# Rounding rows as they come, and three barriers fewer, in layer 1 and block 2 of a two-block transformer kernel

## The reference, cut to what matters

```
br_a = ((a_b * _short_conv(a_c * a_x, conv_w_l)) * silu(a_z)) @ w_br_conv_l
...
return (g_a * br_a + g_b * br_b + g_c * br_c) @ w_out_l
```

```
y = einsum('nbsm,nmd->bsnd', branches, w_branch[layer])
x = x + sum(gate * y, axis=2) @ w_out[layer]
```

## Time and profile before

| | |
|---|---|
| time, median of 3 runs | 4196.48 us (4193.07 to 4197.07) |
| profiled execution | 4197.54 us |
| its span, first to last instruction | 4195.7 us |
| mean granted TensorE clock | 0.955 |
| TensorE busy | 3878.6 us, 92% |
| VectorE, GpSimd, ScalarE busy | 1880.7, 1959.9, 974.4 us |
| layer 1's convolution begins, last matmul | about 2688, 2871 us |
| layer 1's branch product ends | about 2928 us |
| block 2's branch products end | about 3749 us |

### The profile page before, as it was taken

One profiled execution on the slowest core, in us unless ns is written; L12 is line 12 of the kernel. 1 busy time (PEld: TensorE's weight loads), 2 busy tenths in 40 slices (PEclk: granted clock), 3 DMA queues, 4 the chain that ended last, 5 costly groups with the idle time before them and its releaser, 6 DMA issues. The chain is left out here.

```text
span 4195.7 us, 52077 instructions
## 1 busy us (share of the span) xinstructions
PE 3878.6 (92%) x19691; PEld 3083.5 (73%) x19691; DVE 1880.7 (45%) x2716; ACT 974.4 (23%) x1729; POOL 1959.9 (47%) x834
## 2 busy tenths in 40 slices
PE   5999999999989989899999998898898998999999
PEld 4777788888877877576678777676585454877877
DVE  5344326656638882344425655355304555133200
ACT  3333212222210011333312222101214444112200
POOL 2333342332326554244454343687452210887886
PEclk7999999999999999899999999999898998999999
DMA  7211221121225543222222121334422110443433
GB/s 191 49 47 43 74 56 46 44 48 41 52 76 112 117 110 101 60 56 58 75 66 56 44 61 48 90 90 119 128 57 56 38 31 14 95 105 78 96 91 90
DMA packets 481706, 305.17 MB, mean 73 GB/s; under 512 B 37786, under 2 KB 451875, under 8 KB 480635
## 3 DMA queue, kind: packets, MB, share of 16 engines
q1 hardware_dynamic: 469434, 282.43, 28.0%
q10 hardware_dynamic: 12096, 20.33, 1.4%
HBM read 276.42 MB, written 26.27 MB: 72 GB/s over the span
## 5 line engine op out<-in xcount | busy, mean ns | idle before, releaser
L867 POOL TENSOR_TENSOR whi<-ring,con 128x1024 fp32r<-128x1024 f32 (+1 forms) x415 | 978.6, 2358 | 2180.6 <-DMA ring<-in_w_in 1681.4
L551 PE MATMUL ps<-xT_parts,whi 128*128 128x512 f32 (+2 forms) x2632 | 1007.1, 383 | 77.0 <-DVE hT_parts L2099 37.7
L551 PE MATMUL ps<-hT_parts,whi 128*128 128x512 f32 (+1 forms) x2864 | 1049.2, 366 | 0.0
L869 POOL TENSOR_TENSOR ring_parts<-ring,whi 128x1024 fp32r<-128x1024 f32 (+1 forms) x415 | 983.9, 2371 | 32.5
L551 PE MATMUL ps<-xT_parts,ring_parts 128*128 128x512 f32 (+2 forms) x2600 | 944.3, 363 | 0.0
L551 PE MATMUL ps<-arena_parts,whi 128*128 128x512 f32 (+1 forms) x2472 | 765.9, 383 | 74.2 <-DVE arena_parts L2093 63.2
L1551 ACT ACTIVATE arena<-ps 128x512 f32<-128x512 f32 (+7 forms) x583 | 311.5, 544 | 1671.2 <-PE ps L551 960.3
L551 PE MATMUL ps<-arena 128*128 128x128 f32 (+9 forms) x3292 | 647.7, 341 | 27.8 <-DVE arena L2061 22.1
L551 PEld LDWEIGHTS ps<-xT_parts,whi 128*128 128x128 f32 (+1 forms) x2632 | 500.3, 190 | 182.7 <-issue 64.3
L551 PEld LDWEIGHTS ps<-hT_parts,whi 128*128 128x128 f32 x2864 | 544.1, 190 | 91.1 <-issue 7.2
L551 PEld LDWEIGHTS ps<-arena_parts,whi 128*128 128x128 f32 x2472 | 460.0, 194 | 181.4 <-issue 73.9
(11 more groups left out here) (160 smaller groups left out, 3377.1 us busy)
## 6 DMA issues: line engine op xcount, KB each, us to landing
ring<-in_w_in SPq DMA_DIRECT2D x504, 256.0 KB, 4.0
arena<-in_w_ada SPq DMA_DIRECT2D x80, 256.0 KB, 6.2
ring<-in_w_up SPq DMA_DIRECT2D x64, 256.0 KB, 4.0
ring<-in_w_down SPq DMA_DIRECT2D x64, 256.0 KB, 3.6
ring<-in_w_out SPq DMA_DIRECT2D x48, 256.0 KB, 3.8
gates_kept<-stage ACTq DMA_DIRECT2D x24, 384.0 KB, 4.0
arena<-gates_kept SPq DMA_DIRECT2D x24, 384.0 KB, 3.7
ring<-in_w_br_attn SPq DMA_DIRECT2D x32, 256.0 KB, 3.9
```

Source lines behind the costliest of these rows:

```text
L551: return nc.tensor.matmul(o, l, r, start=first, stop=last)
L867: v.tensor_tensor(hi, raw, ones[:, 0:m].unsqueeze(1).to_broadcast([P, kt, m]), ALU.mult).then_inc(w_rounded, 1)
L869: v.tensor_tensor(ringR[:, s, 0:kt, 0:m], raw, hi.bitcast(F32), ALU.subtract).then_inc(w_split, 1)
```

## The change

In layer 1 and in block 2 the activation rows are rounded and subtracted one at a time, as they are made, by new calls in the loops that make them. The barriers `conv1`, `branch0_1` and `branches2` are left out on all engines. The two parts of acc get a place of their own, `acc2P`, in columns of con from `cos` on. VectorE and ScalarE do layer 1's convolution, and block 2's third branch, in written-out loops. SyncE's waits for the barriers become waits for an earlier barrier (gates) and for used weight tiles (x). Layer 0 stays as it is.

```diff
+        acc2P = parts(con[:, C_AT["cos"][0]:C_AT["cos"][0] + KT * LAT].rearrange("p (f n) -> p f n", f=KT), acc)
...
+        acc_row = sem("acc_row")
...
-            def bring_x(before, n, kept):
+            def bring_x(before, n, kept, used=None):
-                sp.wait_ge(phase, 3 * phases_to(before))
+                if before:
+                    sp.wait_ge(phase, 3 * phases_to(before))
+                else:
+                    sp.wait_ge(w_used, used)
...
-                branch(0, a["w_br_conv"][l], f"conv{l}")
+                branch(0, a["w_br_conv"][l], "conv0" if l == 0 else "branch2_1")
...
-                        bring_x(f"branch0_{l}", ALL, l + 1)
+                        bring_x("branch0_0" if l == 0 else None, ALL, l + 1, tiles.number() - 4)
...
-                    bring_x("branches2", LAT, 3)
+                    bring_x(None, LAT, 3, tiles.number() - 4)
```

TensorE:

```diff
-                if phase_end(f"conv{l}"):
+                if l == 0 and phase_end("conv0"):
                     return
                 branch(n)
-                if phase_end(f"branch0_{l}"):
+                if l == 0 and phase_end("branch0_0"):
                     return
-                summed_tiles(accP, n)
+                summed_tiles(accP if l == 0 else acc2P, n)
...
-            if phase_end("branches2"):
-                return
-            summed_tiles(accP, LAT)
+            summed_tiles(acc2P, LAT)
```

ScalarE (`gates_of_conv` is the body of the old loop, `gate2` that of block 2):

```diff
+                def round_row(dst, src, f):
+                    do(dst[0][:, f, 0:n], src[:, f, 0:n], ACT.Copy).then_inc(part_hi, 1)
+                if l == 0:
...
+                else:
+                    for f in range(KT):
+                        gates_of_conv()
+                        if f:
+                            round_row(yP, y, f - 1)
+                    last_read()
+                    round_row(yP, y, KT - 1)
+                    skip(KT)
+                    for f in range(KT):
+                        act.wait_ge(acc_made, KT * (BRANCH_AT[0] + 3 * l) + f + 1)
+                        round_row(acc2P, acc, f)
...
+            def round_row2(f):
+                act.wait_ge(acc_row, f + 1)
+                do(acc2P[0][:, f], acc[:, f, 0:LAT], ACT.Copy).then_inc(part_hi, 1)
+            for b in range(2):
                 with act.Fori(0, KT // 2) as i, tiles.loop(i, KT // 2, 4), uses.loop(i, KT // 2, 4):
                     for s in range(2):
+                        gate2()
+            for f in range(KT):
+                gate2()
+                if f:
+                    round_row2(f - 1)
+            round_row2(KT - 1)
```

VectorE (`conv_row` is the body of the old loop):

```diff
+            def row_rest(dst, src, f, n):
+                parts_made[0] += 1
+                dve.wait_ge(part_hi, parts_made[0])
+                v.tensor_tensor(dst[1][:, f, 0:n], src[:, f, 0:n], dst[0][:, f, 0:n].bitcast(F32),
+                                ALU.subtract).then_inc(part_lo, 1)
-            def branch(b, l, n):
-                keep_rest(yP, y, n)
+            def branch(b, l, n, by_rows=False):
+                if not by_rows:
+                    keep_rest(yP, y, n)
...
+                    if by_rows and f:
+                        row_rest(acc2P, acc, f - 1, n)
+                if by_rows:
+                    row_rest(acc2P, acc, KT - 1, n)
...
+                else:
+                    for f in range(KT):
+                        conv_row(f)
+                        if f:
+                            row_rest(yP, y, f - 1, n)
+                    row_rest(yP, y, KT - 1, n)
...
+            for f in range(KT):
+                skip()
+                p = product()
+                last_read()
+                own.settle()
+                dve.wait_ge(acc_row, f)
+                release(stt(tmp2, tha2, 1.0, bank(2 * p), ALU.add, ALU.mult))
+                last_read()
+                dst = acc[:, f, 0:LAT]
+                stt(dst, tmp2, 0.5, dst, ALU.mult, ALU.add).then_inc(acc_row, 1)
+                if f:
+                    row_rest2(f - 1)
+            row_rest2(KT - 1)
```

More of the change, by code:

```diff
@@ L73 @@
 PHASES = ["load"] + [f"{p}{l}" for l in range(DEPTH)
-                             for p in ("attn", "branch1_", "gla", "branch2_", "conv", "branch0_")] \
-    + ["kv2", "cmp", "heads", "branches2", "up", "down", "end"]
+                             for p in ("attn", "branch1_", "gla", "branch2_", "conv", "branch0_")[:6 if l == 0 else 4]] \
+    + ["kv2", "cmp", "heads", "up", "down", "end"]
 def phases_to(name):
@@ L1852, in _, with gates_of_conv @@
                     return
-                with act.Fori(0, KT) as i, tiles.loop(i, KT, 4), uses.loop(i, KT, 4):
+                def gates_of_conv():
                     p = product()
@@ L1860, in _ @@
                     skip(3)
[L1861 to L1866, removed]
+                def round_row(dst, src, f):
+                    do(dst[0][:, f, 0:n], src[:, f, 0:n], ACT.Copy).then_inc(part_hi, 1)
+                if l == 0:
+                    with act.Fori(0, KT) as i, tiles.loop(i, KT, 4), uses.loop(i, KT, 4):
+                        gates_of_conv()
+                    if phase_end("conv0"):
+                        return
+                    branch(n)
+                    if phase_end("branch0_0"):
+                        return
+                    round_rows(accP, acc, n)
+                else:
+                    for f in range(KT):
+                        gates_of_conv()
+                        if f:
[6 more added lines that the diff above has]
+                        round_row(acc2P, acc, f)
                 for f in range(KT):
@@ L2011, in _, with gate2 @@
             round_rows(y2P, y2, LAT)
-            for b in range(3):
+            def gate2():
+                p = product()
+                last_read()
+                release(do(tha2, bank(2 * p), ACT.Tanh, scale=0.5))
+                skip()
[3 more added lines that the diff above has]
+            for b in range(2):
                 with act.Fori(0, KT // 2) as i, tiles.loop(i, KT // 2, 4), uses.loop(i, KT // 2, 4):
                     for s in range(2):
[L2015 to L2021, removed]
+                        gate2()
[4 more added lines that the diff above has]
+            round_row2(KT - 1)
             for f in range(KT):
@@ L2418, in _, with conv_row @@
                 ns = len(stretches)
-                with dve.Fori(0, KT) as i, tiles.loop(i, KT, 4), uses.loop(i, KT, 4), own.loop(i, KT, 4 * ns + 16 * (l == 0)):
+                def conv_row(i):
                     if l == 0:
@@ L2460, in _ @@
                 if l == 0:
+                    with dve.Fori(0, KT) as i, tiles.loop(i, KT, 4), uses.loop(i, KT, 4), own.loop(i, KT, 4 * ns + 16):
+                        conv_row(i)
+                else:
[4 more added lines that the diff above has]
+                    row_rest(yP, y, KT - 1, n)
+                if l == 0:
                     dve.wait_ge(mod_read, KT)
@@ L2464, in _ @@
                     own(v.tensor_tensor(gpost[:], modl[:, 16:24], over(R_GPOST, 8), ALU.mult))
-                if phase_end(f"conv{l}"):
+                if l == 0 and phase_end("conv0"):
                     return
[L2467 to L2470, removed]
+                branch(0, l, n, l == 1)
+                if l == 0:
+                    if phase_end("branch0_0"):
+                        return
+                    keep_rest(accP, acc, n)
                 skip(8)
@@ L2669, in _, with row_rest2 @@
                             own(stt(dst, tmp2, 0.5, dst, ALU.mult, ALU.add))
-            if phase_end("branches2"):
-                return
+            acc2_from = parts_made[0]
+            parts_made[0] += KT
+            def row_rest2(f):
+                dve.wait_ge(part_hi, acc2_from + f + 1)
+                v.tensor_tensor(acc2P[1][:, f, 0:LAT], acc[:, f, 0:LAT], acc2P[0][:, f].bitcast(F32),
+                                ALU.subtract).then_inc(part_lo, 1)
+            for f in range(KT):
+                skip()
+                p = product()
+                last_read()
+                own.settle()
+                dve.wait_ge(acc_row, f)
+                release(stt(tmp2, tha2, 1.0, bank(2 * p), ALU.add, ALU.mult))
+                last_read()
+                dst = acc[:, f, 0:LAT]
[3 more added lines that the diff above has]
+            row_rest2(KT - 1)
             def residual():
@@ L2678, in _ @@
             add_at = [0]
-            keep_rest(accP, acc, LAT)
             dve.wait_ge(x_back, 48)
```

## The result

| | before | after |
|---|---|---|
| time, median of 4 runs | 4195.36 us (4193.07 to 4197.07) | 4169.89 us (4165.37 to 4172.04) |
| ratio, 95% interval | | 0.9936 (0.9922 to 0.9950) |
| profiled execution, its span | 4197.54, 4195.7 us | 4172.04, 4170.2 us |
| granted TensorE clock, mean | 0.955 | 0.959 |

A forecast was written before the change was run, and what follows sets the result against it. TensorE, busy 92% of the span, bounds the kernel, so gains lie in its standstills and low clock. 8.8 + 9 + 10.5 - 4.5 = 23.8 us off the 4196.5 us median gave 4172.7 us, range 4163 to 4185.

The forecast's parts named there:

- the clock: TensorE's clock falls in the remaining pauses: 2 us lost each at A and C, 0.5 at B, 4.5 together.
- A: Layer 1, convolution to branch product: the first tile, 18.1 us before, ends 8.8 us earlier.
- B: Layer 1, branch product to output product: first tile, 16.3 us before, gains 9 us (9.7, or 6.9 if row 7 misses GpSimd's pause).
- C: Block 2, branch product to output product: the first tile, 20.8 us before, ends 10.5 us earlier.
- Rows 0 to 5 hide: At each barrier, these rows' rounding and subtraction lie beside the stage before and cost nothing; uncovered subtractions would cost 17 to 67 us.
- The convolution's stall, unchanged: TensorE's 4.7 us of waiting for the convolution's last multiply stays; nothing taken, bounds -4 and +5 us.
- x, gates and weights: Loads of gates and x and the weight tiles' splitting bring no new TensorE wait: nothing for any.
- The barriers themselves at nothing: The three barriers are on TensorE's path only through what they hold back, already counted in the three places' sums.
- 1: Rival: the 24 subtractions don't hide, each held 2.8 us by GpSimd; 39 us slower, 4236 us; chance 3%.
- 2: Rival: clock losses of 10 us and GpSimd delays of 7 us take half; 11 us faster, 4185 us; chance 15%.
- 3: Rival: the first tile waits for weights, gates or x instead; 0 to 5 us gained, 4194 us; chance 4%.
- 4: Rival: the convolution's stall goes too and no clock falls; over 33 us gained, 4161 us; chance 6%.

The follow-up runs named there:

- after_again: The kernel after, unchanged, run again in another set: 4179.46 us, 0.9948 of before.
- layer1_alone: Layer 1's part of the change alone, block 2 keeping its barrier and rounding its rows together as in before: 4185.55 us, 0.9973 of before.
- e4: After with the last branches' half products and finished rows, and the convolution's running sum and finished row, in free PSUM banks: 4161.62 us, 0.9907 of before.
- e5: Block 2's part of the change alone, layer 1 as in before with two barriers and rows rounded together: 4185.71 us, 0.9970 of before.
- e7: After with matmuls nobody reads filling TensorE's standstills in the first tiles at A and B: 4176.86 us, 0.9946 of before.
- e1: After, still without the three barriers, but with rows rounded and subtracted together once the last is there: 4195.55 us, 0.9993 of before.
- e2: After with the three barriers put back, rows still rounded as they come: 4191.98 us, 0.9982 of before.
- psum_again: The kernel of e4, unchanged, run again in another set: 4165.32 us, 0.9928 of before.

## Why the prediction was right

The mechanism is the one predicted, but that 23.8 came so near is in part luck. In the terms of my sum the places and the clock gave A 6.4, B 6.7, C 12.0 and the clock -3.0: 22.1 us, and 21.0 over the edited stretches (19.4 in after_again's trace). I had A and B 4.7 us too high together, C 1.5 too low and the clock's loss 1.5 too high, so that the errors nearly cancel; and the 25.5 us of the medians are good to some 6 us. The two sets of after give 26.9 and 21.9 us.

*Rows 0 to 5 hide.* Right: at all three places TensorE went through six rows without a pause. But the cover is thinner than I had it. I gave VectorE at most 5.2 of 5.5 us a tile in the branch product; it takes 5.6, since the add, which took 1.69 us on the mean before, now takes 2.06, and the subtraction 2.88. VectorE and GpSimd have fallen into step, each of VectorE's two instructions waiting out one of GpSimd's, and GpSimd's first operation takes 2.85 us instead of 2.40. The sign that I had named, GpSimd's idle time as before, did not come true: the 0.91 us ahead of w_out's tile are gone, and from 2895 to 2928 us its idle time was 14.8 us in before and 1.8 in after.

*A, 8.8 us.* It gave 5.7, or 6.4 without the low clock of its last three matmuls; 8.2 in the second trace of after and in layer1_alone. My step took the last row's multiply to come where it came in before, 3.1 us behind TensorE; in this trace it came 5.4 us behind, as the chain's instructions each met a GpSimd instruction. These 2.3 us are what the step lacks, and row 6's and row 7's products were late by as much. e4 shows that the holds are the whole rest: without them A is 5.6.

*B, 9 us.* It gave 6.7. The other case that I had named took place, 6.9, row 7's subtraction missing GpSimd's pause. What failed in the step is the pause itself, which I read from the trace before: in step with VectorE, GpSimd no longer has one.

*C, 10.5 us.* It gave 12.0. Row 6's subtraction did not stand where row 0's had stood (4.8 us behind the free TensorE) but 2.3 us behind it (3738.75): the last add took 1.43 us instead of 2.79, and no rounding stood before the subtraction, as row 6 had been rounded a tile earlier, where row 0 waited 0.81 us for ScalarE. In after_again, e5 and e7 C is 9.1 us.

*The clock, 4.5 us.* Too high, and in other places. Against e7's full clock it cost 0.8 behind A and 1.5 behind B. A's first tile ran 1.9 us slower than its 5.55, but only the last three matmuls, 0.7 us, are on the path, as e7 shows: 3.0 us in all. I had put 2 at C, where this trace shows 1.00; in after_again, e5 and e7, with pauses of 1.2 and 1.8 us at C, the clock was low behind them (a mean of 0.75 to 0.78 over the next 7 to 8 us), about 1.7 us each.

*The convolution's stall, unchanged.* 4.7 before, 3.0 in after, 4.4 in the second trace: it wanders with how the chain meets GpSimd, as bounded.

*x, gates and weights.* Right: TensorE missed the pair at C by 0.28 us. e4 shows the margin: C's second tile starts 3.2 us earlier there, and x costs 3.06.

*The barriers themselves at nothing.* e1's 3 us, with an interval that holds no change, agree with it. "Only through what they hold back" is most of the gain, and e2 priced it: 16.1, 17.3 and 16.2 us against 12.4, 9.6 and 8.8, 18.8 us of first tiles in the traces and 14 to 19 us of time.

*Rivals.* 1 fell: no subtraction was on the path in the convolution. 2 had its mechanism in part, GpSimd slower and VectorE full, but nothing of it passed on to TensorE, which found every weight tile split. 3 and 4 did not come; 4's terms (no stall, no low clock) are what e4 then made.

What stays open: the exact worth of the move to PSUM, between 3 and 17 us by the times, and what sets how VectorE's chain meets GpSimd's instructions from trace to trace. Filler products in e2's standstills were not tried.

## What to carry to other kernels

A barrier between two stages that hand over rows costs little by itself and much through what it holds back: round or finish the rows as they come and take the barrier out, since one without the other gave 8 and 3 us of the 22 to 27. Before laying VectorE's work beside GpSimd's, count its instructions with both inputs in SBUF: each may wait out a GpSimd instruction, and one operand in a free PSUM bank took 2.9 us to 0.7. Then look at what comes last next, here the one large transfer of x: until it was split, the move to PSUM won nothing at C.

## What the runs showed of the hardware

- VectorE and GpSimd lock into step: with two held instructions a tile, both engines run without a pause, one tile every 5.6 us, and GpSimd's 128x1024 operation lengthens from 2.40 to 2.85 us.
- A `tensor_scalar` from SBUF to SBUF took 1.36 us on the mean in the convolution and 0.75 to 0.76 into PSUM (traces of e4 and psum_again).
- Filler products (0.23 us each) in standstills of 3.8 us and of 1.7 to 1.8 us kept the granted clock at 1.00, where it had fallen to 0.50; in after's trace standstills of 0.8 and 1.8 us at C left it at 1.00, of 1.7 and 1.8 at B did not, and in after_again's those of 1.2 and 1.8 at C did not either.
- One transfer of 2 MB landed 11.1 to 13.5 us after its issue; as two of 1 MB, issued 0.6 us apart, it landed 8.1 and 12.8 us after.
- Matmuls start 0.231 us apart with both parts in one buffer and 0.233 with the parts in two.
